# The chunk loop of an RWKV-7 branch: scores of the next chunk inside the end of the current one, old-state products between two levels, loops written out

## What is computed

```
def step(s, inp):
    r_t, w_t, k_t, v_t, a_t, b_t = inp
    sa = jnp.einsum('bhij,bhj->bhi', s, a_t)
    s = s * w_t[:, :, None, :] + sa[..., :, None] * b_t[..., None, :] + v_t[..., :, None] * k_t[..., None, :]
    y = jnp.einsum('bhij,bhj->bhi', s, r_t)
    return s, y
```

## Time and profile before

| what | value |
|---|---|
| median of 3 runs | 1297.04 us (1293.07 to 1299.84) |
| the profiled execution, its own time | 1299.64 us |
| its span | 1297.9 us |
| mean granted TensorE clock | 0.946 |
| the chunk stage, first product to last output transfer issued | 273.53 to 539.15 us |
| one chunk to the next, mean of 7 | 31.46 us |

### The profile page before, as it was taken

How to read it: one execution, slowest core, us unless ns; L and a number is a source line. 1 busy time by engine, 2 the same in 40 slices (tenths; PEclk the granted TensorE clock), 3 DMA queues, 4 the chain that set the end, 5 groups by cost and what they waited for, 6 DMA issues and landing times. The chain is left out here.

```text
span 1297.9 us, 24588 instructions
## 1 busy us (share of the span) xinstructions
PE 1150.9 (89%) x10229; PEld 897.1 (69%) x10229; DVE 506.0 (39%) x1186; ACT 314.4 (24%) x617; POOL 181.5 (14%) x189
## 2 busy tenths in 40 slices
PE   3599999958989888799989999999899599988873
PEld 3488888857888888688877788888646355544441
DVE  3135545465555455245554550110135332211125
ACT  2022232235554554300003521000011111111111
POOL 4000000012332332000000002900000122211110
PEclk9799999969998998899999999999998699989997
DMA  3321132020000000122371222260394799999975
GB/s 116 96 60 51 51 85 67 0 69 3 3 3 3 3 3 3 59 66 65 95 194 42 65 65 65 73 206 13 137 419 185 295 387 413 415 417 417 415 315 198
DMA packets 113831, 182.90 MB, mean 141 GB/s; under 512 B 10364, under 2 KB 88520, under 8 KB 105029
## 3 DMA queue, kind: packets, MB, share of 16 engines
q1 hardware_dynamic: 107190, 168.56, 37.0%
q0 software_dynamic: 5168, 8.56, 1.8%
q10 hardware_dynamic: 1383, 4.42, 0.9%
HBM read 173.24 MB, written 17.55 MB: 147 GB/s over the span
## 5 line engine op out<-in xcount | busy, mean ns | idle before, releaser
L271 PE MATMUL rk_ps<-xT,rk_w 128*128 128x260 f32 x768 | 176.0, 388 | 10.0 <-DMA rk_lw<-in_a_lora_up 10.0
L271 PEld LDWEIGHTS rk_ps<-xT,rk_w 128*128 128x128 f32 x768 | 145.9, 192 | 37.5 <-issue 10.1
L271 PE MATMUL mg_psg<-xT,w_merge 128*128 128x260 f32 x512 | 116.5, 386 | 2.7 <-PEq L110 2.7
L271 PEld LDWEIGHTS mg_psg<-xT,w_merge 128*128 128x128 f32 x512 | 98.2, 192 | 18.0 <-issue 2.7
L2028 DVE SCALAR_TENSOR_TENSOR ex_sg<-tl_psA,ex_slot_rs,ex_sg 128x128 f32<-128x128 f32 x32 | 11.2, 351 | 138.8 <-ACT ex_sg L1828 138.6
L848 DVE TENSOR_TENSOR ck_W<-ck_b,levels 128x256 f32<-128x256 f32 x80 | 34.0, 425 | 78.7 <-PE ck_b L608 77.8
L271 PE MATMUL uv_psv<-xT,w_uv 128*128 128x260 f32 x256 | 59.2, 391 | 5.6 <-ACTq L984 5.6
L271 PEld LDWEIGHTS uv_psv<-xT,w_uv 128*128 128x128 f32 x256 | 49.8, 195 | 14.0 <-issue 6.0
L631 POOL TENSOR_TENSOR ck_bk<-br_all,ck_pi 64x512 f32<-64x512 f32 x17 | 21.7, 1274 | 265.2 <-DVEq L816 241.2
L271 PE MATMUL mg_psp<-ya,w_merge 128*128 128x260 f32 x256 | 57.6, 383 | 0.0
L271 PE MATMUL uv_psu<-xT,w_uv 128*128 128x260 f32 x256 | 57.4, 382 | 0.0
(11 more groups left out here) (452 smaller groups left out, 1992.4 us busy)
## 6 DMA issues: line engine op xcount, KB each, us to landing
wd<-in_moe_w_down SPq DMA_DIRECT2D x15, 1024.0 KB, 24.2
rk_w<-in_w_in SPq DMA_DIRECT2D x24, 512.0 KB, 5.2
tl_x<-in_moe_w_down SPq DMA_DIRECT2D x9, 1024.0 KB, 24.5
w_uv<-in_w_in SPq DMA_DIRECT2D x16, 512.0 KB, 5.2
w_merge<-in_w_in SPq DMA_DIRECT2D x16, 512.0 KB, 4.2
xT<-in_moe_w_gate SPq DMA_DIRECT2D x5, 1024.0 KB, 20.1
xT<-in_moe_w_up SPq DMA_DIRECT2D x5, 1024.0 KB, 24.6
bonus_all<-in_moe_w_gate SPq DMA_DIRECT2D x5, 1024.0 KB, 21.5
```

What stands on the lines that cost most here:

```text
L271: last = eng.matmul(out[:, h, 0:TH], weights[:, k, :], xT[:, k, h * TH:(h + 1) * TH], start=(k == 0), stop=(k == NK - 1))
```

## The change

Everything is in `phase_chunks`. The scores are no longer one product per head with 128 columns of weights but two with 64 (four quarters of the array per pair), so that the parts that feed `mb` lie in bank 0 and those that feed `L` in bank 1. `mb` becomes two buffers. The scores of chunk c+1 for group 0 stand on TensorE directly behind the last level of chunk c, and those for group 1 behind the `X` by `rh` products. The old-state products move between the second and the third level; their output part is copied to `m.r` by ScalarE, and the new part is added there later by VectorE. `X` and the copy of the state move from VectorE to GpSimd. `v2` goes: `m.v` is turned in quarters. All loops are written out.

```
-        v2 = sb("ck_v2", [P, NP, 2, CH])
-        mb = sb("ck_mb", [P, NP, P])
+        mbs = [sb(f"ck_mb{n}", [P, NP, P]) for n in range(2)]
...
+            def scores(c, g):
+                b = bank[g]
+                eng.wait_ge(s_ar, c * 4 + 4)
+                eng.wait_ge(s_bk, c * 4 + 4)
+                if c:
+                    eng.wait_ge(s_rh_e[g], 2 * c)
+                    eng.wait_ge(s_w_e[g], c * NL)
+                for n in range(GP):
+                    p = g * GP + n
+                    for rows, which in ((lo, 0), (hi, 1)):
+                        eng.matmul(b4(b[0])[rows, n, :], bk[rows, p, rows], L[rows, p, which, :], start=True, stop=True)
+                    for rows, others, which in ((lo, hi, 0), (hi, lo, 1)):
+                        last = eng.matmul(b4(b[1])[others, n, :], bk[rows, p, others], L[rows, p, which, :],
+                                          start=True, stop=True)
+                last.then_inc(s_eo[g], 1)
...
             for c in range(NC):
                 for g in range(G):
+                    turn_n(c, g)
                 for g in range(G):
+                    turn_bk_v(c, g)
+                level(c, 0)
+                level(c, 1)
                 for g in range(G):
+                    old_state(c, g)
+                for lv in range(2, NL):
+                    level(c, lv)
+                if c + 1 < NC:
+                    scores(c + 1, 0)
                 for g in range(G):
+                    corrected(c, g)
+                if c + 1 < NC:
+                    scores(c + 1, 1)
                 for g in range(G):
+                    new_state(c, g)
```

VectorE's list, with what it waits for at the end of a chunk (`masked_n` writes `mb` in one operation over 128 partitions, `masked_k` a half of `L`):

```
+            def new_state(c, g):
+                eng.wait_ge(s_s[g], c + 1)
+                if c:
+                    eng.wait_ge(s_s0[g], c * 2 + 2)
+                step.did(eng.tensor_tensor(st[:, grp(g), :], b64(bank[g][2]), st[:, grp(g), :], ALU.add))
+                step.wait()
+                eng.tensor_tensor(st[:, grp(g), :], st[:, grp(g), :],
+                                  running(c, CH, CH + 1)[:, grp(g), :].to_broadcast([P, GP, HD]), ALU.mult).then_inc(s_st[g], 1)
+                y = m.r[:, grp(g), tokens(c)]
+                eng.wait_ge(s_y[g], c + 1)
+                eng.wait_ge(s_rh_e[g], c * 2 + 2)
+                eng.tensor_tensor(y, b64(bank[g][3]), y, ALU.add).then_inc(s_y_e[g], 1)
...
+                    if lv == 2 and c + 1 < NC:
+                        eng.wait_ge(s_px, c + 2)
+                        eng.wait_ge(s_rhs[0], c + 1)
+                        eng.wait_ge(s_rhs[1], c + 1)
+                        a_r_rows(eng, c + 1, lo, 0)
+                if c + 1 < NC:
+                    masked_n(c + 1, 0)
+                    masked_k(c + 1, 0, hi, 0)
                 for g in range(G):
+                    corrected(c, g)
+                if c + 1 < NC:
+                    masked_k(c + 1, 0, lo, 1)
+                    masked_n(c + 1, 1)
+                for g in range(G):
+                    new_state(c, g)
+                if c + 1 < NC:
+                    masked_k(c + 1, 1, hi, 0)
+                    masked_k(c + 1, 1, lo, 1)
```

More of the change, by code:

```diff
@@ new lines, in level @@
+            def level(c, lv):
+                for g in range(G):
+                    if lv == 0:
+                        eng.wait_ge(s_a1[g], c + 1)
+                        eng.wait_ge(s_x1[g], c + 1)
+                        eng.wait_ge(s_lk[g], 2 * c + 2)
+                    else:
+                        eng.wait_ge(s_xz_e[g], c * NX + 2 * lv - 1)
+                    own_blocks(eng, b64(bank[g][1]), a1, X, g).then_inc(s_w[g], 1)
+                for g in range(G):
+                    if lv == 0:
+                        eng.wait_ge(s_z1[g], c + 1)
+                        eng.wait_ge(s_tb_e[g], c * 3 + 3)
+                    else:
+                        eng.wait_ge(s_xz_e[g], c * NX + 2 * lv)
+                    eng.wait_ge(s_w_e[g], c * NL + lv + 1)
+                    own_blocks(eng, b64(bank[g][2]), Z, W, g).then_inc(s_xz[g], 1)
+                    if lv < NL - 1:
+                        own_blocks(eng, b64(bank[g][3]), W, Z, g).then_inc(s_xz[g], 1)
@@ new lines, in old_state @@
+            def old_state(c, g):
+                b = bank[g]
+                eng.wait_ge(s_s0[g], c * 2 + 2)
+                for n in range(GP):
+                    p = g * GP + n
+                    eng.matmul(b64(b[0])[lo, n, :], L[:, p, 0, 0:CH], wv[:, p, 0, :], start=True, stop=True)
+                    eng.matmul(b64(b[0])[hi, n, :], L[:, p, 1, 0:CH], wv[:, p, 1, :], start=True, stop=True)
+                for n in range(GP):
+                    p = g * GP + n
+                    eng.matmul(b64(b[0], GP * HD)[lo, n, :], wv[:, p, 0, :], L[:, p, 0, CH:P], start=True, stop=True)
+                    last = eng.matmul(b64(b[0], GP * HD)[hi, n, :], wv[:, p, 1, :], L[:, p, 1, CH:P], start=True, stop=True)
+                last.then_inc(s_rhs[g], 1)
@@ L647, in _ @@
                 for g in range(G):
[L648 to L660, removed]
-                for g in range(G):
[L662 to L675, removed]
@@ L768, in _ @@
                .then_inc(s_sv_e, 1)
-            with eng.Fori(0, NC) as c:
+            for c in range(NC):
+                for g in range(G):
+                    eng.wait_ge(s_nt[g], c + 1)
+                    eng.activation(a1[:, grp(g), :], b64(bank[g][0]), ACT.Copy).then_inc(s_a1[g], 1)
+                for g in range(G):
+                    if c:
+                        eng.wait_ge(s_st[g], c)
+                        eng.wait_ge(s_y[g], c)
+                        eng.activation(wv[lo, grp(g), 0, :], st[lo, grp(g), :], ACT.Copy).then_inc(s_s0[g], 1)
                 for g in range(G):
```

296 lines of the change are left out of this document (136 added, 160 removed).

## The result

| | before | changed |
|---|---|---|
| median | 1295.05 us, 4 runs (1289.37 to 1299.84) | 1250.28 us, 4 runs (1247.19 to 1251.02) |
| ratio, 95% interval | | 0.9651 (0.9607 to 0.9696): faster |
| profiled execution, span | 1299.6, 1297.9 | 1247.19, 1245.1 |

The account below looks back on a forecast made before the run. Levels were taken as bound by TensorE, the turn between chunks as a chain over engines. Chunks of 27.8 us plus start and end gained 30.9, less 5 for low clock: 26, so 1271 us; forecast 1262 to 1283, range 1258 to 1288.

Parts of the forecast that it names:

- VectorE's list is the chain of the new turn: Between a chunk's last level and the next first level, VectorE's operations set the length; level in effect starts at 9.6 us.
- It is not late for VectorE, but only by 0.5: In the turn, TensorE's work beside VectorE's list is ready in time for the first level, with 0.5 us to spare.
- TensorE waiting for it at the first level: Sign that the forecast is right: TensorE waits for VectorE at the first level of a chunk.
- Scores: A group's scores on TensorE become 32 rows instead of 16, at 0.036 us a row: 1.15 us a group.
- The quarters do not overlap: Rival: score quarters with 128 columns take 0.107 us each, eight chunks cost 36 us more, 1307 us; chance 0.06, including similar stalls.
- Collisions: VectorE and GpSimd meeting at SBUF add 0.4 us in the turn (0 to 1.0) and 1.0 in the levels (0.3 to 1.5).
- The rest of the levels: Moved old state costs the same 2.0 us; its copies and the exponentials fit beside the levels on ScalarE.
- A chunk: One chunk takes 14.81 + 2.0 + 1.0 + 9.6 + 0.4 = 27.8 us, against 29.98 at full clock and 31.46 as run.
- The sum: Last transfer at 508.3 instead of 539.15, 30.9 us gained; half the 1.48 low clock stays, 5 us, so gain 26.
- Start: At the stage's start, first scores at about 280.4 and first level at 290.7 instead of 293.69: 3.0 us gained (0 to 5).
- End: From the end of the last level to the last output transfer, 6.2 us behind the old state's 2.0, instead of 10.45.
- More than forecast: Rival: no collision in the levels and no low clock, a chunk of 26.8 us, gain 38, 1259 us; chance 0.09.

Follow-up runs that it names:

- the copies' run: Changed kernel with the two copies of `u` into the upper half of `wv` on ScalarE instead of VectorE; 1248.55 us, ratio to before 0.9662.
- the run with the scores late: Changed kernel with the old state still between the levels, but the next chunk's scores behind the new state; 1276.71 us, ratio to before 0.9867.
- the run with the split: Changed kernel with VectorE's two writes of `L` for the next chunk split over two levels; 1249.89 us, ratio to before 0.967.
- nine needless operations: Changed kernel with nine needless VectorE operations in the turn: in one place 1286.82 us, ratio to before 0.994; in two places 1281.06, 0.989.
- the run with the filler: Kernel before with 32 rows of needless products on TensorE in its 1.4 us pause at a chunk's end; 1292.34 us, ratio 0.9991.

## Why the prediction was wrong, by its steps

The mechanism was right: right place, right chain, right sign, no rival in its stead. What failed is the sum, in the size of its terms, nearly all of them on the same side, so that nothing cancelled. Forecast were 30.9 at full clock less 5 for the clock; the profiled execution gained 47.3 up to the last transfer: 3.4 more at the start, 7 x 1.86 = 13.0 more in the chunks, and no loss of 5. The chunk, forecast at 27.8 and measured at 25.94, is the largest of these.

- *VectorE's list is the chain of the new turn*: right in kind (three more operations cost their 1.25 us). Mis-sized: from the first mask to the first `W` 8.95 with 0.4 of collisions, 9.35, measured 8.18. A small part is arithmetic: by the prices that the prediction names (0.69, 0.425, 0.15) the list adds up to 8.7 and not 8.95; the copies are entered at 0.94 and the two groups' state at 2.94, where the prices give 0.85 and 2.85. The larger part is that durations of single operations were summed, but operations follow each other closer than they last: a mask 0.61 instead of 0.69 where another follows, two copies 0.79 from start to next start. The 0.15 of semaphore twice went with the loops: with the loops alone written out it falls to 0.04.
- "*It is not late for VectorE, but only by 0.5*", of TensorE: measured 0.3, by the copies' run. The sign "TensorE waiting for it at the first level" came half true: TensorE starts the first level's products without a wait (338.89) and waits for VectorE's `W` behind them.
- *Scores*: 1.15 a group forecast, 0.95 measured, 0.03 us a row, the lower bound. The quarters overlap in full, and the rival "The quarters do not overlap" is refuted. The Trainium skill, TensorEngine Tiling (Array Packing), Restrictions and Gotchas, says that different row tiles cannot access the same PSUM bank simultaneously. For this use the trace does not agree: the rows at 638 and 640 come from both row halves, the two that write the same bank write different partitions of it, and the pitch is that of 64x64 products that write two banks.
- *Collisions*: in the turn 0.4 forecast; the two scales last 0.72 and 0.62 instead of 0.426, 0.49 in all, and each ends 0.28 behind the operation of GpSimd that it met; in the last chunk, where they meet none, they last 0.426 and 0.425. In the levels 1.0 forecast, 0.33 measured by splitting the pair (3.48 to 3.15), near the 0.3 that I had as the lower bound. Two things were mis-sized there. The pair on VectorE takes 2.75 (323.13 to 325.89), where I had 3.1 to 3.5 for two collisions; and VectorE's idle time that covers it is 2.27, as the run with the scores late shows it ahead of a `W` with no write before it, where I had 1.95. The Trainium skill, SBUF — State Buffer, in its terms, lets the loser block fully, and by that I had 1.5 for the late `W`. The trace agrees with the rule and not with my use of it: VectorE's first write met the last 0.5 us of GpSimd's and lost 0.4, its second met nearly a whole one and lost 1.1. By my 1.5 it would have lost nearly two whole ones, with less idle time to cover them.
- *The rest of the levels*: old state and exponentials cost what was forecast. The turn, taken as in the prediction from the scores (330.40) to 0.68 ahead of the first `W` (339.80), is 8.72 us. What is left of a chunk, the levels with the old state, is 16.9 in the run with the split (forecast 16.8 without collisions) and 17.2 in the changed kernel (forecast 17.8), the difference being the collision.
- *A chunk*: 27.8 forecast, 25.94 measured: 1.3 less in the turn, 0.6 less in the levels.
- *The sum*, "I let half of the 1.48 us of low clock stay": this step failed by judgement, no row stood behind the half. Not one chunk was low. The split-up shows the clock going in parts: low in every chunk with both moves undone, in four of seven with the old state moved, in none with the scores moved too. And it comes back where TensorE is made to pause again (nine needless operations), though not with a pause of 1.03 us. The pauses that I forecast, 0.2 to 0.8, were shorter than 1.36, the shortest right behind which a run shows it (the scores late, a pause that ends at 402.13, low from 402.28). At 1.48 a chunk 10 us of the profiled gain are this, of which 5 were counted. It is less for a typical execution: in the run with the filler, 1289.38 in its profiled execution, a chunk takes 30.64, 0.66 more than the 29.98 at full clock, or 5 us in seven.
- *Start*: first scores 279.29 (forecast 280.4), first level's products 287.3 (290.7). I carried the 11.0 between the two over from before; it was 8.0. The runs split the 3.0. With the loops alone it is 9.7, and there the clock reaches 1.00 at 286.7, where it did at 291.6 before. With quarters, and the clock at 1.00 from 286.2, it is 8.3 (scores late); in the changed kernel, at 1.00 from 283.3, 8.0. So about half is the clock, with what the loops give, and about half the quarters and what came with them. Why the clock rises earlier is not shown.
- *End*: from the last first-level product (468.9) to the last transfer (491.85) 22.95; forecast 14.8 + 2.0 + 6.2 = 23.0. Right.
- *Loops* at nothing: I had looked only for a cost. They gave 3 us, most of it ahead of the first `W`.
- The rival "More than forecast" had the right direction (no low clock, little collision), with 1259; its chance of 0.09 was too small, and its time too long, since it kept the summed durations. The measured time lies below its band of 1255 to 1261 too.

The later stages moved with the barrier, as forecast, but for the last one: in the profiled pair it took 6 us less (366.0 against 372.3 from the merge's end). That is not the change: in the kernel before with its loops written out, and with the filler, it takes 366 us too, so the 372.3 belongs to the one profiled execution.

## What to carry to other kernels

Cost a chain of short operations by the distance from start to start in a stretch where they already follow each other, not by the sum of their durations, and read a semaphore's gap where the loop stands that will be there after the change. Where a change takes the pauses away behind which the clock was low, price the clock as a term of its own, which can go entirely (here 5 to 10 us), beside the chain. When two engines take turns at SBUF, price the meeting by what is left of the other's operation, and subtract the idle time that covers it. When two engines are within 0.3 us of each other, shortening one gives only that 0.3.

## What the runs showed of the hardware that was not expected

- 64x64 quarters with 128 moving columns that write one bank from both row halves: 32 rows in 0.95 us at full clock, 0.03 a row, as fast as products with half as many columns. At 1.2 GHz (279.29 to the second group at 281.05) the 32 took 1.76, 0.055 a row.
- VectorE's masks start 0.61 behind each other at a duration of 0.68. A pair with a semaphore between has 0.15 of idle time inside a loop on the engine, and 0.04 or less (0.6 us in 16) when it is written out.
- The clock: the same chunk took 28.63 at 1.00 and 30.22 at 0.94. Behind pauses of 3.3 to 3.8 us it fell to 1.2 GHz for 3.4 us, twice for 6.8, in full work; behind pauses of up to 1.25 and 2.00 in one turn, and behind one of 1.94 with the other filled, it fell for 3.4; behind one of 1.03 it did not in any of six turns.
- Two writes of VectorE that read SBUF twice (0.68 alone) and two of GpSimd (1.1 to 1.3 alone) take turns: 1.05 and 1.77 on VectorE, the second of GpSimd 1.75. In each of the fourteen meetings of seven chunks VectorE's write ends 0.54 or 0.55 us behind GpSimd's.
